# Attention's products with 48 keys widened to 112 keys with zeroed probabilities, and the scores of two heads of the gated attention in one group

## The reference

```
s_win  = einsum(qg, k_blk) * scale ;  s_win = where(in_win, s_win + bias, -1e30)
s_meta = einsum(qg, km) * scale
p      = softmax(concatenate([s_win, s_meta]))
o_grid = einsum(p_win, v_blk) + einsum(p_meta, vm)
```

```
q_dec = qf * exp(bcum) ;  k_inv = kf * exp(-bcum)
att   = where(mask, einsum(q_dec, k_inv), 0)        # within a chunk
o     = einsum(att, v) + einsum(q_dec, state)       # state: decayed sum over earlier chunks
```

## Time and profile before

| | us |
|---|---|
| median of 3 runs | 819.37 |
| lowest, highest | 818.33, 821.32 |
| span of the profiled execution, first to last instruction | 817.8 |
| PE busy in it | 803.5 (98%) |
| DVE, ACT, POOL busy | 643.0, 497.9, 123.8 |

### The profile page before, as it was taken

The page is one execution under the profiler, slowest core; times in us unless marked ns, Lnnn a source line. Parts: engine busy times, 40 slices in busy tenths (PEclk is TensorE's granted clock), DMA queues, the critical chain, the costliest instruction groups (busy, mean ns, idle before and its releaser), DMA issues.

```text
span 817.8 us, 17229 instructions
## 1 busy us (share of the span) xinstructions
PE 803.5 (98%) x6996; PEld 787.0 (96%) x6996; DVE 643.0 (79%) x1022; ACT 497.9 (61%) x891; POOL 123.8 (15%) x137
## 2 busy tenths in 40 slices
PE   6999999999999999999999999999999999999996
PEld 6999999989999999999999999999999999999996
DVE  7788599977987878786998898887987568566673
ACT  6575566756677465655666744555676457566652
POOL 0022255401040000000240620001203130000001
PEclk9999999999999999999999999999999999999998
DMA  9934544466667989898777567675765336455441
GB/s 337 382 96 140 165 142 122 154 195 205 194 201 235 355 304 342 305 324 331 249 249 252 164 208 219 216 260 179 207 180 167 127 122 189 177 155 156 149 130 53
DMA packets 47022, 170.42 MB, mean 208 GB/s; under 512 B 5216, under 2 KB 5472, under 8 KB 46688
## 3 DMA queue, kind: packets, MB, share of 16 engines
q1 hardware_dynamic: 46224, 165.31, 61.8%
q10 hardware_dynamic: 720, 4.01, 1.2%
HBM read 168.26 MB, written 1.05 MB: 207 GB/s over the span
## 4 chain that ended last, share of the span: by engine, by line
PE 92%; DVE 4%; ACT 1%; DMA 1%; POOL 1%; issue 0%; SPq 0%; POOLq 0%; DVEq 0%; ACTq 0%
PE bank L196 91%; DVE wl L235 2%; DMA raw<-in_ws 1%; POOL sq L235 1%; DVE raw L223 0%; PE bank L199 0%; ACT wh L205 0%; SPq L193 0%; ACT sq L202 0%; DVE B0l L223 0%; DVE h L223 0%; DVE B1l L235 0%; ACT B1h L202 0%; ACT B0h L202 0%; DVE gd L235 0%
## 5 line engine op out<-in xcount | busy, mean ns | idle before, releaser
L235 DVE TENSOR_TENSOR wl<-raw,wh 128x1024 fp32r<-128x1024 f32 (+1 forms) x260 | 327.6, 1273 | 22.6 <-ACT wh L205 21.5
L205 ACT CAST wh<-raw 128x1024 fp32r<-128x1024 f32 (+1 forms) x260 | 269.0, 1046 | 105.2 <-DMA raw<-in_ws 53.7
L196 PE MATMUL bank<-XAh,wl 128*128 128x256 f32 (+1 forms) x896 | 254.7, 284 | 0.1
L196 PE MATMUL bank<-XAl,wh 128*128 128x256 f32 (+1 forms) x896 | 249.0, 278 | 0.0
L196 PE MATMUL bank<-XAh,wh 128*128 128x256 f32 (+1 forms) x896 | 248.8, 278 | 0.0
L196 PEld LDWEIGHTS bank<-XAh,wl 128*128 128x128 f32 x896 | 168.4, 188 | 3.1 <-issue 1.3
L196 PEld LDWEIGHTS bank<-XAh,wh 128*128 128x128 f32 x896 | 168.6, 188 | 0.1
L196 PEld LDWEIGHTS bank<-XAl,wh 128*128 128x128 f32 x896 | 168.6, 188 | 0.0
L196 PE MATMUL bank<-B1h,wl 128*128 128x256 f32 (+1 forms) x464 | 129.3, 279 | 0.0
L196 PE MATMUL bank<-B1l,wh 128*128 128x256 f32 (+1 forms) x464 | 128.7, 277 | 0.0
L196 PE MATMUL bank<-B1h,wh 128*128 128x256 f32 (+1 forms) x464 | 128.6, 277 | 0.0
(11 more groups left out here) (276 smaller groups left out, 1219.6 us busy)
## 6 DMA issues: line engine op xcount, KB each, us to landing
raw<-in_ws SPq DMA_DIRECT2D x306, 512.0 KB, 4.5
bias<-in_bias ACTq DMA_DIRECT2D x1, 1664.0 KB, 12.0
hK<-in_xk SPq DMA_DIRECT2D x4, 272.0 KB, 5.4
h<-in_xt ACTq DMA_DIRECT2D x1, 1088.0 KB, 7.4
out<-gd SPq DMA_DIRECT2D x4, 256.0 KB, 2.6
raw<-in_ws SPq DMA_DIRECT2D x2, 256.0 KB, 3.9
C<-in_cst SPq DMA_DIRECT2D x1, 512.0 KB, 8.5
crow<-in_crow ACTq DMA_DIRECT2D x1, 512.0 KB, 6.0
```

Of the source, the lines that this page charges most:

```text
L196: return self.real.matmul(*a, **k)
L205: return self.real.copy(*a, **k)
L235: return self.real.tensor_tensor(*a, **k)
```

## The change

First, in the attention products of half b = 0 the contraction runs over rows 0 to 111 of `vM` and `PTm` instead of 64 to 111. So that the 64 new rows add nothing, their probabilities have to be zero: POOL sets them to zero once, early in the program ("pt_zero"), and ACT no longer copies all 112 x 256 elements, but 48 rows for b = 0 and 80 rows for b = 1 with an instruction each. Second, the scores of the gated attention are computed for two heads at one time: first KI and gk of both, then K2 and K3 of both; DVE likewise masks two heads in a row. The products with the values stay where they were.

```diff
-                                z, n = slice(0, 80) if b else slice(64, 112), slice(128 * b, 128 * b + 128)
+                                z, n = slice(0, 80) if b else slice(0, 112), slice(128 * b, 128 * b + 128)
...
+                def scores_of(pair):
+                    ps = [side.take("gs", hh) for hh in pair]
+                    e.wait_ge(*at("gla_keys", pair[0] // 2))
+                    e.wait_ge(*at("gla_far", pair[0] // 2))
+                    for hh in pair:
+                        for n in range(4):
+                            po, co = 64 * (n % 2), 64 * (n // 2)
+                            e.matmul(ps[hh % 2][po:po + 64, co:co + 64], KI[:, hh, 64 * n:64 * n + 64],
+                                     gq[:, hh, 64 * n:64 * n + 64], start=True, stop=True)
+                        e.matmul(ps[hh % 2][0:64, 128:192], gk[:, hh, 0:64], gq[:, hh, 64:128], start=True, stop=True)
+                        e.matmul(ps[hh % 2][0:64, 192:256], gk[:, hh, 128:192], gq[:, hh, 192:256], start=True, stop=True)
+                    for hh in pair:
+                        e.matmul(ps[hh % 2][:, 256:320], K2[:, hh, :], gq[:, hh, 128:192], start=True, stop=True)
+                        e.matmul(ps[hh % 2][:, 320:384], K3[:, hh, :], gq[:, hh, 192:256], start=True,
+                                 stop=True).then_inc(*up("gs", hh))
+                        side.give(("gs", hh), ("gla_at", hh))
+
                 for hh in range(4):
...
+                    if hh % 2 == 0:
+                        scores_of((hh, hh + 1))
                     yield
...
                         e.copy(PT[hh % 3][:, :], ps[:, 0:256])
-                        e.copy(PTm[hh % 3][:, :], ps[0:112, 256:512]).then_inc(*up("turned", hh))
+                        e.wait_ge(*at("pt_zero", hh % 3))
+                        e.copy(PTm[hh % 3][64:112, 0:128], ps[64:112, 256:384])
+                        e.copy(PTm[hh % 3][0:80, 128:256], ps[0:80, 384:512]).then_inc(*up("turned", hh))
...
-                for hh in range(4):
+                def masked(hh):
...
+                for hh in range(4):
+                    if hh % 2 == 0:
+                        masked(hh)
+                        masked(hh + 1)
                     yield
...
+            for i in range(3):
+                if i == 2:
+                    e.wait_ge(*at("sq_sum", 6))
+                e.memset(PTm[i][0:64, 0:128], 0.0).then_inc(*up("pt_zero", i))
```

## The result

The kernel after takes 816.47 us (median of 19 runs, 815.72 to 818.78), the kernel before 819.19 us in the runs beside it (19 runs, 817.74 to 821.32). The ratio is 0.9975, with an interval of 0.9969 to 0.9981: 2.05 us less, 1.6 to 2.5. That is inside half a per cent and counts as no change by the bound of the prediction, but the interval leaves no doubt of the sign. Forecast were 817.5 us and 1.92 us less. (The ratio is not that of the two medians, which differ by 2.7 us.) The profiled execution took 816.05 us, its span is 814.2.

What follows compares the result with a forecast made beforehand. PE was taken to bound the kernel, its time the sum of steps between matmul starts. Attention's 1.20 and gated scores' 0.72 make 1.92 us, taking 819.37 to 817.45, rounded 817.5, range 816.0 to 819.5.

Steps and rivals of the forecast that it cites:

- the bound of the prediction: Whole time: a difference under 0.5%, 4.1 us, cannot be told from no change; chance of landing within it 0.92.
- The bound: Whole kernel: PE, busy 803.5 of 817.8 us, sets the time through the steps between its matmuls' starts.
- Attention, four blocks of 0.30 us: Attention products: steps around the 48-row group fall to 0.11 us, 0.96 becomes 0.66 a block, 1.20 us in all.
- Gated scores, two pairs of 0.36 us: Gated scores: two heads together pay three changes once (0.15 + 0.15 + 0.06), 0.72 us in two pairs.
- Idle of the weight loads: PE weight loads: idle put down to "issue" falls from 28 stretches by eight and by 1.4 us.
- ACT's split copy: ACT in attention: two copies for one add 0.1 us, at worst 0.26, eight times, hidden by 1.98 us before PE's use.
- DVE's masks: DVE at gated scores: two heads' masks in a row, wl some 1.1 us later, head 0's 1.5 us margin grows a little.
- The first (112 rows behave as 48): Attention: 112-row weights wait for products in flight, steps stay 0.16 and 0.21, 0.72 us left, 818.7; chance 0.07.
- The second (gain swallowed where DVE is full): Behind attention, DVE 97% busy: PE idles between 105 and 165 and attention's gain is lost, 818.7; chance 0.08.
- The third (ACT's copies reach PE): Attention: eight extra copies at 0.26, 2.1 us, reach PE undiminished, 819.6, slower than before; chance 0.03.

Runs made afterwards that it cites:

- own order: Kernel after, but each head's K products directly behind its own KI and gk: 817.81 us in one execution, gated stretch 30.50 us.
- before_2: Kernel before, unchanged, timed and profiled again: 818.74 us (11 runs), ratio 0.9996 against its other runs, span 816.2.
- the split alone: Kernel before with the two copies and the zeros, products still over rows 64 to 111: 819.62 us (12 runs), ratio 1.001.
- after_2: Kernel after, unchanged, timed and profiled again beside the kernel before: 817.09 us (11 runs), ratio 0.9982, span 815.7.
- kernel with another number of rows in each block: Kernel after with half b = 0 contracting rows 0 to 47, 0 to 63, 0 to 65, 64 to 111 in the four blocks: 818.57 us, one execution.
- kernel with three repaired places: Kernel after with ATm and iM (32 rows) widened to 128 zeroed rows: 815.73 us (5 runs), ratio 0.9963; again 816.58 us (12 runs), ratio 1.0.

## Why the prediction was right

**The bound.** "The time is the sum of the steps on PE": shown. PE's busy time and the span fell by the same 3.6 us, and no wait on another engine grew.

**Attention, four blocks of 0.30 us.** Mechanism and size right: the block's steps came out at the 0.66 us that was forecast, and the four blocks give 1.15 us for the 1.20 of the forecast (0.29 a block). The six profiles with 48 rows all have 45.21 us from 58 to 103 us; of the seven with 112 rows six have 44.06 and one has 44.15. That products with 112 rows would behave as those with 80 was an inference from two numbers of rows; the blocks with 64 and 66 rows show the limit between them.

**Gated scores, two pairs of 0.36 us.** The sum is right to the second digit, 0.72 for 0.72. Its parts were less so: own order shows that what two heads side by side share, one exit to the main stream, is worth about 0.02 a pair instead of 0.06, and what grouping by form gives is 0.34 a pair instead of 0.30.

**Idle of the weight loads.** Forecast eight stretches and 1.4 us fewer; the view shows ten and 1.8 us fewer. Place by place, the forecast's eight are gone, two in each of the four blocks, 0.17 us each. Of the other two, one stood at 65.96 us, behind the scores that follow the first block: its 0.25 us are still there, at 65.10, and are only put down to DVE's `wl` now. The last stood at 9.1 us, in the start of the program, which the change doesn't touch; the second profile of the kernel before (`before_2`) has none there either.

**ACT's split copy.** This term was mis-sized: taken at 0.1 with an upper bound of 0.26 us per head, measured at 0.29, above the bound. The bound counted one more step of the copy and not that the PT copy, too, now ends with a longer step to what follows it (0.39 for 0.27). Whether the new wait for the zeros or the smaller copy behind it makes that step longer is open, as they came together. It cost nothing because the cover was as named: at the fourth block the copies end at 88.59 and PE takes them at 90.30, 1.7 us later, and the idle of ACT behind is still 1.91 us.

**DVE's masks.** As forecast: two heads in a row, `wl` behind them, and a margin that grows, 1.5 to 1.95 us.

**The rivals.** The first (112 rows behave as 48) fell by the steps of 0.10 to 0.12. The second (gain swallowed where DVE is full) fell because the stretch from attention to the first `AT`, `iN` is 83.57 us before and 83.56 after, with no wait of PE on another engine from 60 to 170 us. The third (ACT's copies reach PE) fell by the split alone: its stretches equal those of the kernel before.

**The time.** The median moved by 2.7 us between the two sets of 19 runs, the ratio by 2.05, and the ratio of the second comparison (`after_2`, 0.9982) by 1.5, for 1.87 us in the traces of what was changed. So the closeness of 2.05 to the forecast's 1.92 is partly luck, as the whole times are no finer than 0.5 us; the stretches are what bears the forecast out. The profile's own 3.6 us is 1.87 of the change, 1.15 of faster main-stream steps that come and go with the execution, and 0.59 of an earlier start. Read alone, the pair of profiles would have credited the change with twice its worth. The forecast's 817.5 was 1.0 above the median, of which 0.2 is the median of the three runs shown (819.37 against 819.19 of the larger set); the rest is of the size of the main stream's two lengths of steps, but how often each kernel's timed runs had which was not to be seen.

## What to carry to other kernels

Where matmuls follow each other without a gap, look at the steps between their starts, not at their durations: a change of the stream into a contraction of 64 rows or fewer, or between 64 and 128 columns of width in the array, cost about 0.15 us here (0.14 to 0.17), and the change back as much. Zeroed rows that lifted a contraction past 64 were free on PE, and grouping small products by form gained where grouping by head alone gave next to nothing (0.68 against 0.04 us). Count the gain some matmuls behind the place: at the products with 32 rows a part of it was given back there. A change worth a few tenths of a per cent is read from stretches of the trace that both kernels share; ratios of whole times were good to about 0.001 here, and one pair of profiles held 1.7 us that had nothing to do with the change.

## What the runs showed that was not expected

The main stream's steps have two lengths at one and the same granted clock of 1.00: 0.113 and 0.118 us, held over tens of us, without any wait in the trace. Between 458 and 518 us they were worth 1.15 us. In the kernel with another number of rows in each block they stood between 206 and 252 us instead, where no other profile had them; the same window there and in the kernel after:

```profile
206.00:250.00 44.00, 44.00 (x376) 44.00 (x375) 36.34 (x59) 28.27 (x50) 8.46 (x7) 1.00 0.61 192
```

```profile
206.00:250.00 44.00, 44.00 (x389) 43.95 (x388) 36.79 (x61) 30.00 (x54) 8.48 (x7) 1.00 0.64 197
```

Thirteen matmuls fewer in 44 us; that stretch explains 1.7 us of that kernel's longer span. Not every slow stretch goes with the execution: the short ones behind the widened products with 32 rows are in both profiles of that kernel and in no other. What sets the length of the steps stays open: the clock, the waits and the share of DMA are equal or nearly so, and no experiment here was made to find its cause.

The limit between 64 and 66 rows is sharp: two more rows take 0.3 us off a block. And the four executions near 823 us of the kernel with three repaired places are unexplained.
